# Selecting matmuls between modulation products, an early first weight unit, two-engine modulation, and one load of the function table ahead of the experts

## The reference, cut to what matters

```
mod(c)  = silu(c) @ w_mod[i] + b_mod[i]      -> sh1, sc1, g1, sh2, sc2, g2     (for x)
mod(cc) = silu(c_ctx) @ w_mod[0] + b_mod[0]  -> csh1, csc1, ...                (for the context)
layer 0: h  = x   * (1 + sc1)  + sh1         hc = ctx * (1 + csc1) + csh1
         q, k, v = h @ w_qkv ;  k_c, v_c = hc @ w_qkv[:, Q_DIM:]
         x  = LN(alpha*x + g1 * (windowed attention with context keys @ w_o))
         x  = LN(alpha*x + g2 * (silu(h @ w1) * (h @ w3)) @ w2)
layer 1: short gated convolution, then 8 experts, each token in its top 2:
         y_e = (silu(x_e @ w1[e]) * (x_e @ w3[e])) @ w2[e]
```

## Time and profile before

| | |
|---|---|
| median of 3 runs | 2552.37 us (2550.55 to 2554.25) |
| the profiled execution, its own time | 2551.86 us |
| its span in the trace | 2550.1 us |
| PE busy | 2309.6 us, 91% of the span |
| DVE busy | 1509.1 us, 59% |
| ACT busy | 1115.8 us, 44% |
| granted PE clock, mean | 0.948 of full |
| DMA | 514.62 MB, mean 202 GB/s |

### The profile page before, as it was taken

The page is one execution under the profiler, slowest core; times in us unless marked ns, Lnnn a source line. Parts: engine busy times, 40 slices in busy tenths (PEclk is TensorE's granted clock), DMA queues, the critical chain, the costliest instruction groups (busy, mean ns, idle before and its releaser), DMA issues.

```text
span 2550.1 us, 38310 instructions
## 1 busy us (share of the span) xinstructions
PE 2309.6 (91%) x14692; PEld 2024.5 (79%) x14693; DVE 1509.1 (59%) x1340; ACT 1115.8 (44%) x1075; POOL 346.6 (14%) x211
## 2 busy tenths in 40 slices
PE   5999979999987996698999999999999999999990
PEld 4866757887875875588999999988888889998880
DVE  3456565434476445487444444468888884445886
ACT  3135432222223223476333433357777774334771
POOL 0000118888560000100000000000000000000004
PEclk7989989999998996799999999999999999999995
DMA  6420155554431211788544545468898885545873
GB/s 279 182 83 1 71 230 194 183 183 149 179 116 66 99 66 50 268 335 303 187 180 174 200 180 183 181 243 329 335 346 325 345 334 209 190 171 197 313 279 132
DMA packets 76452, 514.62 MB, mean 202 GB/s; under 512 B 8272, under 2 KB 8400, under 8 KB 19056
## 3 DMA queue, kind: packets, MB, share of 16 engines
q1 hardware_dynamic: 61632, 444.55, 46.7%
q0 software_dynamic: 14768, 69.35, 7.4%
HBM read 484.51 MB, written 29.36 MB: 202 GB/s over the span
## 4 chain that ended last, share of the span: by engine, by line
PE 82%; DVE 10%; issue 3%; ACT 2%; DMA 2%; POOL 0%; DVEq 0%; ACTq 0%; SPq 0%; POOLq 0%
PE ps L1427 25%; PE ps L1429 24%; PE ps L1428 24%; DVE lo L1001 3%; PE ps L540 2%; PE ps L495 2%; PE ps L551 2%; PE ps L1665 1%; DVE hl L1352 1%; DMA raw<-w_mod 1%; PE ps L499 1%; PE ps L1468 1%; DMA xg<-dispatched_x 0%; DVE xz L1097 0%; DVE rstd L1091 0%
## 5 line engine op out<-in xcount | busy, mean ns | idle before, releaser
L1001 DVE TENSOR_TENSOR lo<-raw,hi 128x2048 fp32r<-128x2048 f32 x397 | 928.4, 2357 | 214.4 <-ACT hi L767 212.1
L767 ACT ACTIVATE hi<-raw 128x2048 fp32r<-128x2048 f32 x397 | 760.0, 1914 | 507.2 <-PE ps L1429 497.9
L1427 PE MATMUL ps<-hi,xth 128*128 128x256 f32 x2464 | 706.1, 287 | 13.8 <-DVE xtl L1332 12.9
L1429 PE MATMUL ps<-hi,xtl 128*128 128x256 f32 x2464 | 700.0, 284 | 0.0
L1428 PE MATMUL ps<-lo,xth 128*128 128x256 f32 x2464 | 699.9, 284 | 0.0
L1427 PEld LDWEIGHTS ps<-hi,xth 128*128 128x128 f32 x2464 | 475.3, 193 | 25.3 <-DVE xtl L1332 14.3
L1428 PEld LDWEIGHTS ps<-lo,xth 128*128 128x128 f32 x2464 | 475.5, 193 | 1.9
L1429 PEld LDWEIGHTS ps<-hi,xtl 128*128 128x128 f32 x2464 | 475.3, 193 | 0.0
L1427 PE MATMUL ps<-ah,hi 128*128 128x512 f32 x688 | 272.4, 396 | 19.2 <-DVE al L1063 12.9
L1427 PE MATMUL ps<-hi,hh 128*128 128x512 f32 x616 | 248.8, 404 | 28.9 <-DVE hl L1352 28.9
L1428 PE MATMUL ps<-al,hi 128*128 128x512 f32 x688 | 270.7, 393 | 0.0
(11 more groups left out here) (230 smaller groups left out, 2490.7 us busy)
## 6 DMA issues: line engine op xcount, KB each, us to landing
raw<-w_moe SPq DMA_DIRECT2D x338, 1024.0 KB, 4.8
raw<-w_pre SPq DMA_DIRECT2D x59, 1024.0 KB, 4.8
raw<-w_mod POOLq DMA_DIRECT2D x28, 1024.0 KB, 5.1
raw<-w_mod SPq DMA_DIRECT2D x20, 1024.0 KB, 7.2
dispatched_x<-zt POOLq DMA_DIRECT2D x22, 512.0 KB, 15.0
xg<-dispatched_x POOLq DMA_DIRECT2D x8, 1024.0 KB, 5.8
expert_y<-ys POOLq DMA_DIRECT2D x8, 1024.0 KB, 5.6
expert_y<-zt POOLq DMA_DIRECT2D x6, 512.0 KB, 24.6
```

The lines of the kernel that those rows point to most:

```text
L767: act.activation(HI[h][:], RAW[r][:], ACT.Copy).then_inc(hi_ready[h], 1)
L1001: dve.tensor_tensor(LO[h][:], RAW[r][:], HI[h][:].bitcast(F32), ALU.subtract).then_inc(raw_used[r], 1)
L1427: pe.matmul(outp, wh, ah, start=first, stop=False, skip_group_check=True)
L1429: return pe.matmul(outp, wl, ah, start=False, stop=last, skip_group_check=True)
```

## The change

It has four parts, and none changes a result beyond rounding.

- **Loads and selecting matmuls.** SP issues six `w_mod` units, the context, the first `w_pre` unit, and then the last two `w_mod` units; the mask goes behind x. PE runs the four selecting matmuls of a row one pair of units later, so that two of the four groups stand ahead of the last two units.
- **First weight unit early.** ACT splits `w_pre` unit 0 before it copies the last `mp` row, DVE makes its low part before it waits for `mod_full`.
- **Two-engine modulation.** ACT no longer copies DVE's `tmp`: it makes `cxh` and `ah` itself from `cx` and `xz`, with scale and bias read from `cg`, `coef` and `mod`, and DVE makes its `tmp` beside it. For the context, DVE too now begins the next `tmp` before the last low part. ACT waits for DVE's last `tmp` of x before it overwrites x by alpha*x, and copies the mask after that. PE takes each context piece as its `cxl` arrives, both column blocks of a piece after each other.
- **Function table.** The request for Silu stands once, ahead of the loop over the experts.

The diff, cut to its core:

```
@@ SP
-            for u in range(MOD_A):
+            for u in range(6):
                 load(u % 4, w_mod[u])
-            sp.dma_start(MASKF[:], maskin[:, 1, :]).then_inc(mask_in, 16)
             sp.dma_start(CX[:], ctxT_in).then_inc(cxin, 16)
             load(0, w_pre[0])
+            for u in (6, 7):
+                load(u % 4, w_mod[u])
             sp.dma_start(XZ[:], xT_in).then_inc(xin, 16)
+            sp.dma_start(MASKF[:], maskin[:, 1, :]).then_inc(mask_in, 16)
             load(1, w_pre[1])
@@ ACT
-            for p in range(MOD_A // 2):
+            def mod_row(p):
                 act.wait_ge(raw_used[2 * (p % 2) + 1], 2 + p // 2)
                 act.activation(MP[p][:], PS[:, p, :], ACT.Copy).then_inc(mrow_ready, 1)
+            for p in range(3):
+                mod_row(p)
...
+            full_split(0, 0)
+            mod_row(3)
...
-            act.wait_ge(idr_ready, 2)
+            act.wait_ge(cxin, 16)
+            act.wait_ge(cg_ready, 1)
             for k in range(KD):
-                act.wait_ge(ctx_tmp, k + 1)
-                act.activation(CXH[:, k, :], TMP[k % 2][:, 0:CTX], ACT.Copy).then_inc(cxh_ready, 1)
...
-            full_split(0, 0)
+                act.activation(CXH[:, k, :], CX[:, k, :], ACT.Identity, bias=MOD[:, 1, k:k + 1],
+                               scale=CG[:, k:k + 1]).then_inc(cxh_ready, 1)
+            act.wait_ge(xin, 16)
             for k in range(KD):
-                to_hi(k)
+                act.activation(AH[:, k, :], XZ[:, k, :], ACT.Identity, bias=MOD[:, 0, k:k + 1],
+                               scale=COEF[:, 0, 0, k:k + 1]).then_inc(ah_ready, 1)
+            cnt["tmp"] += KD
+            act.wait_ge(tmp_ready, KD)
             for k in range(KD):
                 act.activation(XZ[:, k, :], XZ[:, k, :], ACT.Copy, scale=ALPHA).then_inc(alpha_done, 1)
...
+            act.wait_ge(mask_in, 16)
+            act.activation(MASK[:], MASKF[:], ACT.Copy).then_inc(idr_ready, 1)
...
             def expert_round(r):
-                act.preload_act_table(ACT.Silu)
                 for q in range(4):
...
             per_e = times(per_g, GROUPS)
+            act.preload_act_table(ACT.Silu)
             with t.loop(act, NE, per_e) as e:
@@ DVE
+            split(0, 0)
             dve.wait_ge(mod_full, t.n("mod"))
...
-            for k in range(KD):
-                if k >= 2:
-                    dve.wait_ge(cxl_ready, k - 1)
-                dve.tensor_scalar(TMP[k % 2][:, 0:CTX], CX[:, k, :], CG[:, k:k + 1], MOD[:, 1, k:k + 1],
-                                  ALU.mult, ALU.add).then_inc(ctx_tmp, 1)
...
+            for k in range(KD + 1):
+                if k < KD:
+                    if k >= 2:
+                        dve.wait_ge(cxl_ready, k - 1)
+                    dve.tensor_scalar(TMP[k % 2][:, 0:CTX], CX[:, k, :], CG[:, k:k + 1], MOD[:, 1, k:k + 1],
+                                      ALU.mult, ALU.add).then_inc(ctx_tmp, 1)
+                if k >= 1:
+                    dve.wait_ge(ctx_tmp, k)
+                    dve.wait_ge(cxh_ready, k)
+                    dve.tensor_tensor(CXL[:, k - 1, :], TMP[(k - 1) % 2][:, 0:CTX], CXH[:, k - 1, :].bitcast(F32),
+                                      ALU.subtract).then_inc(cxl_ready, 1)
...
-            split(0, 0)
             dve.wait_ge(xin, 16)
@@ PE
-            for u in range(MOD_A):
-                mod_unit(u % 4, PS[:, u // 2, (u % 2) * 256:(u % 2 + 1) * 256])
...
+            for p in range(MOD_A // 2 + 1):
+                if p < MOD_A // 2:
...
+                    for j in range(2):
+                        mod_unit((2 * p + j) % 4, PS[:, p, j * 256:(j + 1) * 256])
+                if p >= 1:
+                    pe.wait_ge(mrow_ready, p)
+                    for c in range(4):
+                        at = 2 * (4 * (p - 1) + c)
+                        ins = pe.matmul(PS[:, 7, at:at + 2], MP[p - 1][:, c * P:(c + 1) * P], SEL[:], start=True,
+                                        stop=True, skip_group_check=True)
...
-            pe.wait_ge(cxl_ready, KD)
...
-                            for c in range(2):
-                                for k in range(KD):
+                            for k in range(KD):
+                                pe.wait_ge(cxl_ready, k + 1)
+                                for c in range(2):
                                     three(PS[:, 2, c * CTX:(c + 1) * CTX], hi[:, k, c * P:(c + 1) * P],
```

More of the change, by code:

```diff
@@ L268, in program @@
         mod_free = sem("mod_free")
-        silp_zero, sel_ready, alpha_done = sem("silp_zero"), sem("sel_ready"), sem("alpha_done")
+        silp_zero, sel_ready, alpha_done, cg_ready = map(sem, ("silp_zero", "sel_ready", "alpha_done", "cg_ready"))
         dve_step = sem("dve_step")
@@ L785, in _ @@
             act.activation(IDR[:], ident, ACT.Copy).then_inc(idr_ready, 1)
-            for p in range(MOD_A // 2):
+            def mod_row(p):
                 act.wait_ge(raw_used[2 * (p % 2) + 1], 2 + p // 2)
                 act.activation(MP[p][:], PS[:, p, :], ACT.Copy).then_inc(mrow_ready, 1)
+            for p in range(3):
+                mod_row(p)
+            for r in range(4):
+                t.skip(("raw", r), 2)
+            full_split(0, 0)
+            mod_row(3)
             def mod_part(e):
@@ L795, in mod_part @@
                 act.activation(MP[e][:], PS[:, 6, :], ACT.Copy).then_inc(mrow_ready, 1)
-            act.wait_ge(mask_in, 16)
-            act.activation(MASK[:], MASKF[:], ACT.Copy).then_inc(idr_ready, 1)
             cnt = {"tmp": 0}
@@ L810, in scale_x @@
                                scale=COEF[:, stage, 2, k:k + 1]).then_inc(xz_ready, 1)
-            act.wait_ge(idr_ready, 2)
+            act.wait_ge(cxin, 16)
+            act.wait_ge(cg_ready, 1)
             for k in range(KD):
-                act.wait_ge(ctx_tmp, k + 1)
-                act.activation(CXH[:, k, :], TMP[k % 2][:, 0:CTX], ACT.Copy).then_inc(cxh_ready, 1)
-            for r in range(4):
-                t.skip(("raw", r), 2)
-            full_split(0, 0)
+                act.activation(CXH[:, k, :], CX[:, k, :], ACT.Identity, bias=MOD[:, 1, k:k + 1],
+                               scale=CG[:, k:k + 1]).then_inc(cxh_ready, 1)
+            act.wait_ge(xin, 16)
             for k in range(KD):
-                to_hi(k)
+                act.activation(AH[:, k, :], XZ[:, k, :], ACT.Identity, bias=MOD[:, 0, k:k + 1],
+                               scale=COEF[:, 0, 0, k:k + 1]).then_inc(ah_ready, 1)
+            cnt["tmp"] += KD
+            act.wait_ge(tmp_ready, KD)
             for k in range(KD):
@@ L1029, in _ @@
             dve.tensor_scalar(COEF[:, 0, 0, :], modcol(0, 1), 1.0, None, ALU.add)
-            step(dve.tensor_scalar(CG[:], MOD[:, 1, 8:16], 1.0, None, ALU.add))
+            dve.tensor_scalar(CG[:], MOD[:, 1, 8:16], 1.0, None, ALU.add).then_inc(cg_ready, 1)
+            dve.wait_ge(cg_ready, 1)
             dve.wait_ge(cxin, 16)
-            for k in range(KD):
-                if k >= 2:
-                    dve.wait_ge(cxl_ready, k - 1)
-                dve.tensor_scalar(TMP[k % 2][:, 0:CTX], CX[:, k, :], CG[:, k:k + 1], MOD[:, 1, k:k + 1],
-                                  ALU.mult, ALU.add).then_inc(ctx_tmp, 1)
-                dve.wait_ge(ctx_tmp, k + 1)
-                dve.wait_ge(cxh_ready, k + 1)
-                dve.tensor_tensor(CXL[:, k, :], TMP[k % 2][:, 0:CTX], CXH[:, k, :].bitcast(F32),
-                                  ALU.subtract).then_inc(cxl_ready, 1)
+            for k in range(KD + 1):
[9 more added lines that the diff above has]
+                                      ALU.subtract).then_inc(cxl_ready, 1)
             nt = [0]
@@ L1470, in mod_unit @@
                 ins.then_inc(raw_used[r], 1)
-            for u in range(MOD_A):
-                mod_unit(u % 4, PS[:, u // 2, (u % 2) * 256:(u % 2 + 1) * 256])
             pe.wait_ge(sel_ready, 1)
             pe.wait_ge(mod_free, t.n("mod"))
-            for p in range(MOD_A // 2):
-                pe.wait_ge(mrow_ready, p + 1)
-                for c in range(4):
-                    at = 2 * (4 * p + c)
-                    ins = pe.matmul(PS[:, 7, at:at + 2], MP[p][:, c * P:(c + 1) * P], SEL[:], start=True, stop=True,
-                                    skip_group_check=True)
+            for p in range(MOD_A // 2 + 1):
+                if p < MOD_A // 2:
+                    if p == MOD_A // 2 - 1:
+                        t.skip(("raw", 0), 1)
+                    for j in range(2):
[6 more added lines that the diff above has]
+                                        stop=True, skip_group_check=True)
             ins.then_inc(mod_full, 1)
+            t.skip(("raw", 0), -1)
             def mod_pair(e):
@@ L1536, in _ @@
                             pair(1)
[L1537 to L1538 removed]
+                            for k in range(KD):
+                                pe.wait_ge(cxl_ready, k + 1)
+                                for c in range(2):
```

(2 more changed lines are left out.)

1 line of the change is left out of this document (removed).

## The result

| | before | after |
|---|---|---|
| median of 4 runs, us | 2552.11 (2550.55 to 2554.25) | 2529.41 (2527.73 to 2531.81) |
| profiled execution, us | 2551.86 | 2528.51 |
| its span, us | 2550.1 | 2526.5 |

The ratio is 0.9911, with a 95% interval of 0.9894 to 0.9928: 22.7 us faster. The prediction was 2529.0, range 2521 to 2538.

The account below looks back on a forecast made before the run. PE was taken to bound the kernel, busy for 91% of the span. Gains of 9.8 (head), 7.7 (table) and 5.6 (clock) sum to 23.1 us, from 2551.86 to 2528.8, by the median 2529; range 2521 to 2538.

Parts of the forecast that it names:

- The two loads ahead of units 6 and 7: +5.0: Head: two 1 MB loads put ahead delay `w_mod` units 6 and 7 by 5.0 us; last unit starts at 30.5.
- Unit 7 and the selecting groups at half clock, `mod` at 35.9: Head: unit 7 ends at 32.4, two selecting groups at half clock take 3.5 us, `mod_full` comes at 35.9.
- From `cg` to the second `w_pre` unit: 23.3: Head: DVE's pieces, alpha, mask and split put the second `w_pre` unit 23.3 us behind `cg`, at 59.7 instead of 69.47.
- The end that the prediction named: Head: gain only 6 us if loads are 2 us later still and the new wait brings a half-clock stretch.
- its bound of 31: Head: splitting the first `w_pre` unit early costs nothing as long as that unit lands before 31.
- The table: 7.7: Expert rounds: without the load PE's wait for `xtl` falls from 2.15 to 0.87 in six rounds, 7.7 us.
- nothing else is late then: Round starts: without the load, DVE copies its `ys` half beside ACT's before the first `xth` and is free for `xtl`.
- DVE's copy of `ys` takes the table's place: Rival: in the rounds the wait moves, and the head's gain is lost later; gain under 5, 2548 to 2552, chance 3%.
- The clock behind the wait: 5.6: Expert rounds: all four falls of the granted clock behind the `xtl` waits go, 1.4 us each, 5.6 us.
- The sum: Whole kernel: 9.8 + 7.7 + 5.6 = 23.1 us gained, giving 2529.
- 9.8 stood: Head: second `w_pre` unit starts 9.8 us earlier, and the shift passes through whole; ends 6 and 14.8.
- The slower rival: Rival, expert loop: table loaded again for each of 14 Silus a round, 90 us in five one-tile rounds; 2632, chance 2%.

Follow-up runs that it names:

- pe_waits_all: Changed kernel, but PE waits for all eight `cxl` pieces before its first context matmul; 2531.22 us, one execution.
- head_only: Changed kernel with the function table load put back at the start of every round; 2541.62 us, ratio to before 0.9959.
- ys_late: Changed kernel with ACT's and DVE's copies of a round's `ys` behind the next round's first `xth` and `xtl`; 2530.81 us, ratio 0.9919.
- other_table: Changed kernel with two table loads, Exp's then Silu's, at the start of every round; 2555.80 us, one execution.
- old_loads: Changed kernel with SP's loads in the order of before: eight `w_mod` units, context, first `w_pre` unit; 2527.96 us, one execution.
- best: `ys_late` plus SP's order of `w_mod` 6 and 7, `w_pre` 0, context after six `w_mod` units; 2525.31 us, ratio 0.9902.
- best2: `best` with half of the clearing of the y accumulator moved from DVE to ACT; 2520.11 us, ratio 0.9879.
- table_only: Kernel before with only the function table load moved, one load ahead of the experts; 2539.63 us, ratio 0.9954.
- both_undone: Changed kernel with both ACT's direct form and DVE's new context order undone; 2539.60 us, one execution.
- act_copies: Changed kernel with ACT again copying DVE's `tmp` into `cxh` and `ah`, DVE's new order kept; 2533.12 us, one execution.

## Why the prediction was right

*The two loads ahead of units 6 and 7: +5.0.* Right. Unit 7 started 4.88 us later (30.39, forecast 30.5), and in eight other traces with that order of loads at 30.2 to 31.2.

*Unit 7 and the selecting groups at half clock, `mod` at 35.9.* In the profiled execution of after this term was too large: the selecting groups took 1.95 us, not 3.5, and `mod` came at 33.83. But the other traces show that both happen. Of nine kernels whose loads stand in this order, two ran those groups in 1.95 us (after and `pe_waits_all`) and seven in 3.57 or 3.58 at half clock, with `mod` at 35.7 to 36.7. This is `head_only`:

```profile
31.19 1.94 PE L1482 MATMUL ps<-raw,silp 128*32 128x256 f32 x16 [0.54 <-DMA raw<-w_mod]
33.05 3.58 PE L1498 MATMUL ps<-sel,mp 128*128 128x2 f32 x16
```

So the forecast was the commoner case, and the head's gain against before's 69.47 is 11.8 us in one and 8.9 to 9.9 in the other: the second unit stands at 59.56 in `ys_late`, 59.97 in `other_table` and 60.56 in `head_only`. What decides between them stays open; nothing in the kernel before that point differs. That after's kept trace shows the rarer case is chance.

*From `cg` to the second `w_pre` unit: 23.3.* Right, and the firmest number of the case: 23.57 to 23.59 in every trace that has the change's context (after, `old_loads`, `head_only`, `ys_late`, `other_table`, `best`, `best2`), whatever came before. Its chain is DVE's 0.79 a piece, 1.18 a piece of x, alpha, mask, high and low part, and the wait in front of the unit, forecast near 1, is 0.68 in after and 0.82 to 2.03 in the six others. The end that the prediction named, a fall of the clock behind this new wait, came once: in `other_table`, behind the 2.03 us, the granted clock was 0.65 over the next 4.3 us. The first split, which the prediction had done by 28.3, ended at 29.62, still ahead of its bound of 31.

*The table: 7.7.* Too high by 0.9. Behind three rounds the wait fell by 1.42, more than the load, since `xth` now even starts 0.1 before the end of `ys`. Behind the other three, one-tile rounds, it fell only by 0.86: there DVE's copy of `ys` (1812.08 to 1813.29) stands behind two low parts, and `xtl` waits for it. In before DVE had stood idle for only 0.78 us between that copy and `xtl`, so the load of 1.28 us could not be won whole. I had written that nothing else is late then, and that DVE's copy ends beside ACT's. That step of the prediction failed, though its sum did not suffer much; it is the rival "DVE's copy of `ys` takes the table's place", in half of the rounds and for 0.56 us. Timeline of DVE at such a round, in before:

```profile
1829.95 1.22 DVE L1359 COPY ys<-ps 128x1024 f32<-128x1024 f32 x1
1831.94 2.48 DVE L1332 TENSOR_TENSOR xtl<-ps,xth 128x512 fp32r<-128x512 f32 x4 [0.78 <-ACT xth L939]
```

and of ACT and DVE at the same round, in after:

```profile
1811.10 1.03 ACT L966 ACTIVATE ys<-ps 128x1024 f32<-128x1024 f32 x1 [1.82 <-PE ps L1443]
1812.02 2.06 ACT L949 ACTIVATE xth<-ps 128x512 fp32r<-128x512 f32 x4
1812.08 1.21 DVE L1373 COPY ys<-ps 128x1024 f32<-128x1024 f32 x1
1813.21 2.47 DVE L1346 TENSOR_TENSOR xtl<-ps,xth 128x512 fp32r<-128x512 f32 x4
```

*The clock behind the wait: 5.6.* Right: all four falls are gone. The forecast reasoned from an idle time of 0.83 us; that 1.29 would leave the clock alone too did not follow from it. Both terms together were forecast at 13.3; from the start of the first round's transposes to the end of the last group the time fell by 12.7 us (1433.7 to 1421.0), and `table_only` by itself shows 13.0 (1420.7).

*The sum.* 23.1 forecast, 23.6 in spans: 12.0 at the experts' start where 9.8 stood, 12.7 in the rounds where 13.3 stood, and about 1 us given back behind the last round (PE's wait for DVE's `dg` is 11.5 instead of 10.5; in `head_only`, `ys_late` and `best`, which have the same code there, it is 10.4 or 10.5, so it is not the change's doing). The median's 22.7 is the better number for the change. That it lies 0.4 us from the forecast is luck: the mechanism was right, but the head stood 2 us above its term by the clock, the table 0.9 below its own, and `dg` took 1 us back.

*The slower rival* (a table load for each Silu) did not come: after its single load at 1019.78 no other stands among the experts. The Trainium skill, page "ScalarE: Activation LUTs", section "What ACT_TABLE_LOAD costs", gives 2.66 us for a switch of sets; the switches of `other_table` took 1.28 each, with the next ACTIVATE 0.01 us behind, so by the trace there is no drain to be saved here. The loads that the change removes asked for the set that was already in place, and took the same 1.28 us.

## What to carry to other kernels

Count a gain from the point where two engines hand over for good, here `cg`: the chain behind it (23.6 us) held in all seven kernels that left it as it is, while what lay before it varied by 2 us with the clock. When a fixed piece of work goes out of a handover, ask which engine is next and how full it is: taking the table away showed DVE's copy, putting that copy elsewhere showed DVE's low part, and only taking work off DVE helped, by 2.8 us in the rounds. When an idle time of PE shrinks, look at the granted clock behind it as well: here waits of 0.73 and 1.29 us cost their own length, and four of six waits of 2.15 us cost another 1.4 us each. And read a term of 2 us from more than one trace: the kernel before alone reached its second `w_pre` unit at 69.47 in one execution and at 67.48 in another.

## What the runs showed of the hardware that was not expected

- The granted clock at the same place of the same instruction stream differs from one execution to another: 16 selecting matmuls of 128 x 2 took 1.95 us twice and 3.57 or 3.58 us seven times. By contrast, the falls behind the six waits of 2.15 us came in the same four rounds in before and in `head_only`.
- The length of an idle time does not settle by itself whether the clock falls. Ahead of the second `w_pre` unit PE stood idle 2.03 us in `other_table`, and the clock was 0.65 over the next 4.3 us; 2.86 us in `both_undone` and 1.92 in `act_copies`, and it stayed at 1.00. In the rounds none of 48 waits of 0.7 to 1.3 us lowered it.
- Loading Exp's table and then Silu's took 1.28 us each, the same as loading Silu's when it was in place.
